# A recurrence stage written one projection ahead, with its first two projections in half pieces and 360-column third pieces

## The chip, the cores and the metric

The kernel runs on one core of a Trainium2 chip. The metric is the device time of one launch in microseconds (us); lower is better. Matmuls run on TensorE (PE), elementwise work on VectorE (DVE), ScalarE (ACT) and GpSimd (POOL), and transfers are issued from the queues of SyncE (SP) and of ACT.

## What is computed

One layer of a hybrid decoder for 1024 prompt tokens and 8 sequences of 8 sample tokens, width 1024. The part that matters here is the first branch:

```
xn = rms_norm(x, norm_g)
proj = jnp.einsum('btd,dn->btn', xn, w_in)
x_lru, z_lru, q, k, v, z_gla, a_lo, gate_logits = jnp.split(proj, IN_SPLITS, axis=-1)
xc, conv_new = causal_conv(x_lru, conv0, conv_w, conv_b)
# rg_lru: r, i = sigmoid(block-diagonal maps of xc); a = exp(-8 r softplus(-lam))
# h_t = a_t h_(t-1) + sqrt(1 - a_t^2) (i_t xc_t)
y_a = jnp.einsum('btw,wd->btd', h.astype(dt) * jax.nn.silu(z_lru), w_lru_o)
```

A gated linear attention branch, a merge of the two, an output projection and a last norm follow. They are untouched, except that their projections use the same helper `piece`.

## The kernel before

**Layout.** Channels lie on the 128 partitions, tokens along the free dimension: 1088 tokens, padded to 1092, in 3 pieces of 364 columns. A projection ("job") makes 128 output channels for all tokens. Each fp32 operand is kept as a high and a low part, so a job is 3 pieces x 8 k-steps x 3 products (L455 to L457) = 72 matmuls. There are 72 jobs: 16 in the recurrence stage, 16 in the first merge stage, 24 in the attention, 16 after it. Only 16 of the jobs, x(i) and z(i) for the 8 channel blocks i, belong to the recurrence stage.

**Weights.** Of each weight block, ACT makes the high part (`hi`, L817, semaphore hi_ok) and POOL the low part (`lo`, L423, semaphore lo_ok); there are two slots, even jobs in slot 0 and odd ones in slot 1. POOL runs its program in order: `lo(0, 0)` for x(0), then the masks and constants of the attention (L429 to L444), then `lo(0, 1)` for z(0), then the rest in a loop.

**Start.** For nine tiles of tokens ACT squares and takes the root (L827, L830), DVE scales (L1133), PE transposes (`x_transpose`, L482, 8 per tile), ACT and DVE split into high and low (L837, L1124). PE runs in order; between the transposes it puts pieces of x(0). z(0) starts after x(0) is complete.

**Recurrence stage.** Two banks of three PSUM slots: bankA for x(i) and then the r gate, bankB for z(i) and then the i gate. PE per block: z(i), gates(i) (two gates of 9 matmuls, L455 to L457 on xcs), x(i+1). The gates need the convolution of x(i): ACT copies x(i) out of bankA (`evacuate`, L860 to L862), DVE convolves (L1186, L1189), ACT and DVE split the result (L870, L1197). DVE also copies z(i) out (L1199). Then come the tanhs, decay, root, scan (L874 to L886, L1201 to L1229) of block i.

## Time and profile before

| | us |
|---|---|
| median of 3 runs | 1186.61 |
| lowest and highest | 1181.58, 1188.57 |
| the profiled execution, its own time | 1186.15 |
| its span, first to last instruction | 1184.4 |
| TensorE busy within the span | 1149.3 |

TensorE is busy nearly throughout; the recurrence stage takes from about 43 us to 259 us. A row of the timeline gives start, duration, engine, line, operation, and in brackets how long the engine was idle before and what ended that. Matmuls overlap in their recorded durations, so the rate of a run of matmuls is the distance of their starts.

### The profile page before, as it was taken

To read this page: it belongs to the slowest core of one execution; us is meant where nothing else is said; L and a number is where in the kernel's file an instruction comes from. 1 tells how busy PE (TensorE), PEld (TensorE's weight loads), DVE (VectorE), ACT (ScalarE), POOL (GpSimd) and SP (SyncE) were. 2 spreads that over 40 slices of the span, in tenths; PEclk is the share of its full clock that TensorE was granted. 3 is DMA by queue.
4 is the path that set the end of the run, shared out by engine and by line. 5 is a ranking of instruction groups with operands and counts; after the bars stand their busy time and mean duration, and the time that the engine had idled before them with its cause. 6 is when DMAs were issued, how large, how long until landed. Compare 5 with 4: busy or idle time off the path is not lost.

```text
span 1184.4 us, 17796 instructions
## 1 busy us (share of the span) xinstructions
PE 1149.3 (97%) x6888; PEld 1108.4 (94%) x6888; DVE 540.2 (46%) x711; ACT 423.5 (36%) x557; POOL 199.2 (17%) x128
## 2 busy tenths in 40 slices
PE   5899999999999999999999999999999999999997
PEld 5899999999999999999999999999989999999886
DVE  5777777775000001662395357438534002444332
ACT  5555555554111112542543453345434111122211
POOL 3511111111212120210112011111202121120000
PEclk8999999999999999998999999999999999999999
DMA  6211111111211222210311131031002103432331
GB/s 210 65 41 49 48 40 40 40 36 37 91 55 54 72 75 64 68 37 18 112 35 35 35 95 35 18 96 52 18 18 80 49 18 110 154 117 90 107 106 54
DMA packets 95488, 76.18 MB, mean 64 GB/s; under 512 B 3928, under 2 KB 88792, under 8 KB 95464
## 3 DMA queue, kind: packets, MB, share of 16 engines
q1 hardware_dynamic: 84444, 61.59, 17.5%
q10 hardware_dynamic: 11020, 14.26, 3.5%
q8 instruction: 16, 0.26, 0.1%
q14 instruction: 8, 0.07, 0.0%
HBM read 62.04 MB, written 13.80 MB: 64 GB/s over the span
## 4 chain that ended last, share of the span: by engine, by line
PE 88%; issue 6%; DVE 3%; ACT 2%; DMA 0%; DVEq 0%; ACTq 0%
PE ps L455 26%; PE ps L456 25%; PE ps L457 25%; PE ps L590 2%; PE ps L653 1%; PE ps L632 1%; PE ps L624 1%; PE ps L634 1%; PE ps L617 1%; DVE xcs L1197 1%; PE ps L672 1%; ACT xcs L870 1%; PE ps L561 1%; DVE xc L1189 1%; PE ps L581 1%
## 5 line engine op out<-in xcount | busy, mean ns | idle before, releaser
L455 PE MATMUL ps<-xn,whi 128*128 128x364 f32 x1344 | 451.9, 336 | 1.7 <-DVE xn L1124 1.5
L456 PE MATMUL ps<-xn,whi 128*128 128x364 f32 x1344 | 443.1, 330 | 0.0
L457 PE MATMUL ps<-xn,wlo 128*128 128x364 f32 x1344 | 442.7, 329 | 0.0
L423 POOL TENSOR_TENSOR wlo<-raw,whi 128x1024 fp32r<-128x1024 f32 x72 | 180.9, 2513 | 860.6 <-ACT whi L817 860.6
L455 PEld LDWEIGHTS ps<-xn,whi 128*128 128x128 f32 x1344 | 254.0, 189 | 6.1 <-issue 2.5
L456 PEld LDWEIGHTS ps<-xn,whi 128*128 128x128 f32 x1344 | 254.2, 189 | 0.2
L457 PEld LDWEIGHTS ps<-xn,wlo 128*128 128x128 f32 x1344 | 253.7, 189 | 0.0
L817 ACT ACTIVATE whi<-raw 128x1024 fp32r<-128x1024 f32 x72 | 76.0, 1056 | 151.6 <-PE ps L457 85.9
L456 PE MATMUL ps<-act_s,whi 128*128 128x364 f32 x384 | 126.2, 329 | 0.0
L455 PE MATMUL ps<-act_s,whi 128*128 128x364 f32 x384 | 126.2, 329 | 0.0
L457 PE MATMUL ps<-act_s,wlo 128*128 128x364 f32 x384 | 126.1, 329 | 0.0
L1245 DVE SCALAR_TENSOR_TENSOR keep<-keep,ps 128x1092 f32 x7 | 9.0, 1292 | 146.6 <-PE ps L457 146.6
L1427 DVE TENSOR_TENSOR wos<-woraw,wos 128x1024 f32 (+1 forms) x8 | 18.4, 2304 | 124.3 <-ACT wos L1078 124.3
L457 PEld LDWEIGHTS ps<-act_s,wlo 128*128 128x128 f32 x384 | 72.2, 188 | 0.0
L456 PEld LDWEIGHTS ps<-act_s,whi 128*128 128x128 f32 x384 | 72.2, 188 | 0.0
L455 PEld LDWEIGHTS ps<-act_s,whi 128*128 128x128 f32 x384 | 72.1, 188 | 0.0
L456 PE MATMUL ps<-wos,whi 128*128 128x512 f32 x144 | 56.0, 389 | 0.0
L455 PE MATMUL ps<-wos,whi 128*128 128x512 f32 x144 | 56.0, 389 | 0.0
L457 PE MATMUL ps<-wos,wlo 128*128 128x512 f32 x144 | 56.0, 389 | 0.0
L1308 DVE COPY_PREDICATED att<-lmask,ps 128x256 f32<-128x256 uint16 x56 | 26.1, 531 | 25.1 <-PE ps L590 25.1
L1107 ACT ACTIVATE junk<-yy 128x1024 f32<-128x1024 f32 (+1 forms) x9 | 9.5, 1060 | 75.9 <-DVE yy L1469 75.9
L1189 DVE SCALAR_TENSOR_TENSOR xc<-xbuf,vec,xc 128x1024 f32<-128x1024 f32 (+1 forms) x48 | 34.6, 779 | 0.0
(230 smaller groups left out, 1367.2 us busy)
## 6 DMA issues: line engine op xcount, KB each, us to landing
raw<-in_w_in SPq DMA_DIRECT2D x56, 512.0 KB, 3.8
branch_a<-keep ACTq DMA_DIRECT2D x8, 546.0 KB, 2.8
mal<-branch_a SPq DMA_DIRECT2D x8, 544.0 KB, 4.6
xt<-in_x_prompt SPq DMA_DIRECT2D x8, 512.0 KB, 6.8
raw<-in_w_lru_o SPq DMA_DIRECT2D x8, 512.0 KB, 3.6
st<-in_state_gla ACTq DMA_DIRECT2D x4, 1024.0 KB, 5.5
out<-st ACTq DMA_DIRECT2D x4, 1024.0 KB, 4.7
raw<-in_w_gla_o SPq DMA_DIRECT2D x8, 512.0 KB, 5.7
```

What stands on the lines that cost most here:

```text
L423: pool.tensor_tensor(wlo[:, c % 2], raw[:, c % 2], whi[:, c % 2].bitcast(F32), ALU.subtract).then_inc(s["lo_ok"], 1)
L455: pe.matmul(dst, wh, mh, start=first, stop=False)
L456: pe.matmul(dst, wh, ml, start=False, stop=False)
L457: return pe.matmul(dst, wl, mh, start=False, stop=last)
L561: ins = pe.matmul(ps[0:2 * RANK, bankA + j, 0:PIECE], aw[:, k, :], xn[:, r, k, j * PIECE:(j + 1) * PIECE], start=(k == 0 and r == 0), stop ...
L581: ins = pe.matmul(ps[:, b, c * P:(c + 1) * P], kb[:, cols], qb[:, cols], start=True, stop=True)
L590: ins = pe.matmul(ps[:, b, i * P:(i + 1) * P], qk[:, l % 2, 2 * i * P:(2 * i + 1) * P], qk[:, l % 2, (2 * i + 1) * P:(2 * i + 2) * P], sta ...
L617: ins = pe.transpose(ps[0:nr, b, (n % 4) * P:(n % 4 + 1) * P], src[:, n * P:n * P + nr], ident[:, :])
L817: act.activation(whi[:, c % 2], raw[:, c % 2], ACT.Copy).then_inc(s["hi_ok"], 1)
L1189: ins = dve.scalar_tensor_tensor(dst, src, wk, dst, ALU.mult, ALU.add)
L1308: ins = dve.copy_predicated(dst, mask, src)
L1427: dve.tensor_tensor(wos[:, 1, 2 * i + j, :], woraw[:, :], wos[:, 0, 2 * i + j, :].bitcast(F32), ALU.subtract).then_inc(s["wo_lo"], 1)
```

## The change

PE's order per block becomes x(i+1), gates(i), z(i+1), with the i gate ahead of the r gate in the loop; ACT and DVE follow with functions for each part, called for block i and i+1 in turn. The last block is written out after the loop, on ACT as z_tanh(7), decay_root(6), hi, r_gate_tanh(7), i_gate_tanh(7). The copy of z out of PSUM is gone: ACT's tanh and DVE's silu read bankB directly. At the start PE interleaves half pieces of x(0) and z(0) with the transposes; the loads of the small rows move from SP's queue to ACT's; z(0)'s weights are loaded and split (`hi(0, 1)`) earlier. POOL's program is the same. The third piece of every job and gate has 360 columns in place of 364.

```diff
+        def columns(j):
+            return slice(j * PIECE, min((j + 1) * PIECE, NTOK))
...
@@ sync
-            sp.wait_ge(s["pad_ok"], 1)
-            row(R_CONVW, t["conv_w"][0])
...
+            sp.wait_ge(s["x_sq"], 1)
+            load_x(4)
+            sp.dma_start(raw[:, 1], w_in[:, :, COL_Z:COL_Z + P]).then_inc(s_raw[1], 16)
+            for n in range(5, TTILES):
...
@@ tensor
-            x_transpose(4)
-            pe.wait_ge(s["lo_ok"], 1)
-            piece(0, bankA, xn, 0)
+            FIRST, SECOND = range(KT // 2), range(KT // 2, KT)
+            pe.wait_ge(s["x_lo"], 3)
+            pe.wait_ge(s["lo_ok"], 1)
+            piece(0, bankA, xn, 0, FIRST)
+            x_transpose(4)
+            piece(0, bankA, xn, 0, SECOND)
             x_transpose(5)
+            pe.wait_ge(s["lo_ok"], 2)
+            piece(1, bankB, xn, 0, FIRST)
             x_transpose(6)
+            piece(1, bankB, xn, 0, SECOND)
+            x_transpose(7)
             pe.wait_ge(s["x_lo"], 6)
-            piece(0, bankA, xn, 1, range(KT // 2))
-            x_transpose(7)
+            piece(0, bankA, xn, 1, FIRST)
             x_transpose(8)
-            piece(0, bankA, xn, 1, range(KT // 2, KT))
+            piece(0, bankA, xn, 1, SECOND)
+            pe.wait_ge(s["x_lo"], TTILES - 1)
+            piece(1, bankB, xn, 1)
             pe.wait_ge(s["x_lo"], TTILES)
...
             piece(0, bankA, xn, 2).then_inc(s["job_done"], 1)
+            piece(1, bankB, xn, 2).then_inc(s["job_done"], 1)
...
             with pe.Fori(0, KT - 1) as i:
-                z_and_gates(i)
-                pe.wait_ge(s["r_tanh"], i + (ONE + 1))
+                pe.wait_ge(s["x_evac"], i + 1)
+                pe.wait_ge(s["r_tanh"], i + ONE)
                 job(i, N_LRU + 2, bankA, xn)
-            z_and_gates(KT - 1)
+                gate_pair(i, i + 2, (1, 0))
+                pe.wait_ge(s["i_tanh"], i + (ONE + 1))
+                job(i, N_LRU + 3, bankB, xn)
+            gate_pair(KT - 1, KT, (0, 1))
...
@@ scalar
+            act.wait_ge(s["pad_ok"], 1)
+            row(R_CONVW, t["conv_w"][0])
...
+                if n == 3:
+                    hi(0, 1)
...
+            def act_step(i):
+                act.wait_ge(s["job_done"], 2 * i + 3)
+                evacuate_x(i + 1)
+                i_gate_tanh(i)
+                r_gate_tanh(i)
+                hi(i, 4)
+                gate_hi(i + 1)
+                decay(i)
+                conv_hi(i + 1)
+
+            with act.Fori(0, KT - 2) as i:
+                act_step(i)
+                decay_root(i)
+                z_tanh(i + 1)
+                hi(i, 5)
+            act_step(KT - 2)
+            z_tanh(KT - 1)
+            decay_root(KT - 2)
+            hi(KT - 2, 5)
+            r_gate_tanh(KT - 1)
+            i_gate_tanh(KT - 1)
+            decay(KT - 1)
+            decay_root(KT - 1)
...
@@ vector
+            with dve.Fori(0, KT - 2) as i:
+                gated_input(i)
+                conv(i + 1)
+                input_scale(i)
+                conv_lo(i + 1)
+                recurrence(i, sz)
+                z_silu(i + 1, sz)
+            gated_input(KT - 2)
+            conv(KT - 1)
+            conv_lo(KT - 1)
+            input_scale(KT - 2)
+            z_silu(KT - 1, tz)
+            recurrence(KT - 2, sz)
+            gated_input(KT - 1)
```

**First place: PE at the start.** Before, with the semaphores that a row waits for (lo_ok counts the low weight parts from POOL, x_scaled and x_lo the token tiles; a 128x364 matmul row opens a run of them):

```order
L492 MATMUL ps<-ident,rows 128x44 [waits rows_in]
...
L482 MATMUL ps<-ident,xt 128x128 [waits x_lo,x_scaled]
L482 MATMUL ps<-ident,xt 128x128 x7
L455 MATMUL ps<-xn,whi 128x364 [waits lo_ok]
...
L455 MATMUL ps<-xn,whi 128x364 [waits x_lo]
...
L482 MATMUL ps<-ident,xt 128x64 [waits x_lo,x_scaled]
...
L455 MATMUL ps<-xn,whi 128x364 [waits pad_ok,x_lo]
```

The same stretch after the change, where the second row with lo_ok is the first one of z(0):

```order
L490 MATMUL ps<-ident,rows 128x44 [waits rows_in]
...
L453 MATMUL ps<-xn,whi 128x364 [waits lo_ok,x_lo]
...
L480 MATMUL ps<-ident,xt 128x128 [waits x_lo,x_scaled]
L480 MATMUL ps<-ident,xt 128x128 x7
L453 MATMUL ps<-xn,whi 128x364 [waits lo_ok]
...
L453 MATMUL ps<-xn,whi 128x364 [waits x_lo]
...
L480 MATMUL ps<-ident,xt 128x64 [waits x_lo,x_scaled]
...
L453 MATMUL ps<-xn,whi 128x360 [waits vec_ok,pad_ok,x_lo]
```

The wait for z(0)'s low weights (the second lo_ok) moved from behind all nine transposes and all of x(0) to ahead of the transposes 6, 7 and 8 and of two thirds of x(0).

**Second place: PE in the loop of the recurrence stage.** Before, from the gates (xcs) of block i to x(i+1):

```order
L455 MATMUL ps<-xcs,ghi 128x364 [waits g_lo,xc_lo]
...
L455 MATMUL ps<-xcs,ghi 128x364 [waits z_copy]
...
L468 REGISTER_ALU [waits r_tanh]
L455 MATMUL ps<-xn,whi 128x364 [waits lo_ok]
...
L526 COMPARE_AND_BRANCH
```

After, one turn of the loop, x(i+1), the gates, and z(i+1):

```order
L466 ISA [waits r_tanh,x_evac]
L453 MATMUL ps<-xn,whi 128x364 [waits lo_ok]
...
L527 REGISTER_ALU [waits g_lo,xc_lo]
L453 MATMUL ps<-xcs,ghi 128x364 [waits z_silu]
...
L453 MATMUL ps<-xcs,ghi 128x364 [waits r_tanh,x_evac]
...
L466 REGISTER_ALU [waits i_tanh]
L453 MATMUL ps<-xn,whi 128x364 [waits lo_ok]
```

x(i+1) moved between the evacuation of x(i) and the gates that need its convolution; the second gate now waits for the evacuation of x(i+1).

**Third place: ACT at the end of the stage.** Before, the last turn of the loop is like every other (tr and ti are the gates' tanhs, xcs the high part of the convolution, wt<-wt the root):

```order
L870 ACTIVATE xcs<-xc 128x1092 [waits conv_step]
L816 REGISTER_ALU [waits raw_in1]
L817 ACTIVATE whi<-raw 128x1024 [waits job_done]
L874 ISA [waits r_done,dvec_ok]
L874 ACTIVATE tr<-ps,dvec 128x1092
```

After, from the high part of block 7's convolution to the tanh of its r gate:

```order
L894 ACTIVATE xcs<-xc 128x1092 [waits conv_step]
L900 ACTIVATE tz<-ps 128x1092 [waits z_silu,job_done]
L921 ACT_TABLE_LOAD
L921 ACTIVATE wt<-wt 128x1092 [waits w_ok]
L828 ACTIVATE whi<-raw 128x1024 [waits job_done,raw_in1]
L910 ACT_TABLE_LOAD
L910 ACTIVATE tr<-ps,dvec 128x1092 [waits r_done]
```

The tanh of z, the root of block 6 and two table loads now stand ahead of the tanh of block 7's r gate.

## Rows read from the trace of the kernel before

**Rows 1.** The page, busy time and share of the span, engine PE

```profile
PE 1149.3 (97%) x6888; PEld 1108.4 (94%) x6888; DVE 540.2 (46%) x711; ACT 423.5 (36%) x557; POOL 199.2 (17%) x128
```

**Rows 2.** Timeline of PE, one turn of the loop: start us, duration us, operation

```profile
88.29 0.32 PE L456 MATMUL ps<-xn,whi 128*128 128x364 f32 x1
...
111.91 0.33 PE L457 MATMUL ps<-xn,wlo 128*128 128x364 f32 x1
113.20 0.43 PE L455 MATMUL ps<-xcs,ghi 128*128 128x364 f32 x1 [0.96 <-DVE xcs L1197]
...
116.14 0.33 PE L457 MATMUL ps<-xcs,glo 128*128 128x364 f32 x1
116.46 0.43 PE L455 MATMUL ps<-xn,whi 128*128 128x364 f32 x1
```

**Rows 3.** Timeline of ACT, the same turn

```profile
100.44 1.28 ACT L860 ACT_TABLE_LOAD   x1 [5.12 <-PE ps L457]
101.74 0.78 ACT L860 ACTIVATE xbuf<-ps 128x728 f32<-128x728 f32 x1
...
102.71 0.23 ACT L862 ACTIVATE xbuf<-ps 128x64 f32<-128x64 f32 x1
...
116.61 1.17 ACT L877 ACTIVATE ti<-ps,dvec 128x1092 f32<-128x1092 f32 x1 [0.28 <-PE ps L457]
...
122.67 1.12 ACT L886 ACTIVATE wt<-wt 128x1092 f32<-128x1092 f32 x1 [0.20 <-DVE wt L1207]
```

**Rows 4.** Windows, that turn: PE, PEld, DVE, ACT, POOL busy us, clock, DMA

```profile
84.70:113.20 28.50, 27.48 (x162) 26.88 (x162) 21.04 (x27) 14.07 (x16) 4.81 (x2) 1.00 0.15 41
```

**Rows 5.** Timeline of POOL and DVE at the start

```profile
17.11 2.97 POOL L423 TENSOR_TENSOR wlo<-raw,whi 128x1024 fp32r<-128x1024 f32 x1 [13.92 <-ACT whi L817]
...
22.52 1.29 DVE L1133 SCALAR_TENSOR_TENSOR xt<-xt,rstd,ngb 128x1024 f32<-128x1024 f32 x1
...
22.68 1.23 POOL L430 TENSOR_SCALAR_AFFINE_SELECT lmask<-lmask 128x64 bf16<-128x64 bf16 x1
```

**Rows 6.** Timeline of POOL, the low weight part of z(0)

```profile
40.80 2.41 POOL L423 TENSOR_TENSOR wlo<-raw,whi 128x1024 fp32r<-128x1024 f32 x1
```

**Rows 7.** Timeline, DVE and ACT at the start; ACT queue at 463 us

```profile
1.12 0.91 DVE L1115 MEMSET rows<- 44x1024 f32 x1 [0.18 <-issue]
...
6.22 1.06 ACT L827 ACTIVATE junk<-xt 128x1024 f32<-128x1024 f32 x1 [3.45 <-DMA xt<-in_x_prompt]
...
15.98 1.04 ACT L817 ACTIVATE whi<-raw 128x1024 fp32r<-128x1024 f32 x1
...
463.46 2.70 ACTq L963 DMA_DIRECT2D wa_raw<-in_w_a  x6
```

**Rows 8.** Timeline of PE at the start

```profile
24.19 0.51 PE L456 MATMUL ps<-xn,whi 128*128 128x364 f32 x1
24.49 0.51 PE L457 MATMUL ps<-xn,wlo 128*128 128x364 f32 x1
...
28.59 1.91 PE L482 MATMUL ps<-ident,xt 128*128 128x128 f32 x16
...
43.27 0.43 PE L455 MATMUL ps<-xn,whi 128*128 128x364 f32 x1 [0.20 <-POOL wlo L423]
```

**Rows 9.** Windows of PE: stretch, busy us, granted clock, DMA share, GB/s

```profile
26.40:26.60 0.20, 0.20 (x3) 0.63 0.00 0
1180.00:1181.00 1.00, 0.00 (x0) 0.63 0.00 0
```

**Rows 10.** Timeline of PE, the end of the stage: last z(7), first merge projection

```profile
254.17 0.33 PE L457 MATMUL ps<-xn,wlo 128*128 128x364 f32 x1
...
258.64 0.43 PE L455 MATMUL ps<-xn,whi 128*128 128x364 f32 x1
```

**Rows 11.** Timeline of PE, matmuls of 512 columns, the output projection

```profile
1099.98 0.39 PE L456 MATMUL ps<-wos,whi 128*128 128x512 f32 x1
...
1102.93 0.39 PE L457 MATMUL ps<-wos,wlo 128*128 128x512 f32 x1
```

More of the change, by code:

```diff
@@ L230, in build, with part_of @@
         bankA, bankB = 0, 3
-        bankX, bankR = (3, 6), 5
+        bankX, bankR = (slice(6, 8), slice(4, 6)), 2
+        def columns(j):
+            return slice(j * PIECE, min((j + 1) * PIECE, NTOK))
+        def part_of(b, j):
+            return ps[:, b + j, 0:columns(j).stop - columns(j).start]
         def slot3(b):
@@ L324, in _ @@
         def _(sp):
-            def row(r, ap):
-                sp.dma_start(rows[r:r + ap.shape[0], 0:ap.shape[1]], ap).then_inc(s["rows_in"], 16)
             def load_x(n):
@@ L507, in _, with gate_pair @@
             piece(0, bankA, xn, 2).then_inc(s["job_done"], 1)
-            pe.wait_ge(s["vec_ok"], 1)
-            def z_and_gates(i):
-                pe.wait_ge(s["i_tanh"], i + ONE)
-                job(i, N_LRU + 1, bankB, xn)
+            piece(1, bankB, xn, 2).then_inc(s["job_done"], 1)
+            def gate_pair(i, evacuated, gates):
                 pe.wait_ge(s["xc_lo"], i + 1)
                 pe.wait_ge(s["g_lo"], i + 1)
-                for g, b in ((0, bankA), (1, bankB)):
-                    if g == 1:
-                        pe.wait_ge(s["z_copy"], i + 1)
+                for g in gates:
+                    b = (bankA, bankB)[g]
+                    if g == 0:
+                        pe.wait_ge(s["x_evac"], evacuated)
+                        pe.wait_ge(s["r_tanh"], i + ONE)
+                    else:
+                        pe.wait_ge(s["z_silu"], i + (ONE + 1))
@@ L1115, in _ @@
             dve.memset(rows[:, :], 0.0).then_inc(s["pad_ok"], 1)
-            dve.memset(xn[:, :, :, NTOK:TOK].bitcast(F32), 0.0).then_inc(s["pad_ok"], 1)
+            dve.memset(xn[:, :, :, NTOK:TOK].bitcast(F32), 0.0)
+            dve.memset(ps[:, bankA + 2:bankB + 3:3, NTOK - 2 * PIECE:PIECE], 0.0).then_inc(s["pad_ok"], 1)
             dve.wait_ge(s["ng_in"], 16)
```

96 lines of the change are left out of this document (60 added, 36 removed).

## The prediction

> **What bounds the kernel now.** I read the busy shares first: TensorE (PE) is busy 97% of the span, no other engine half of it [rows 1]. So a change gains only where PE stands still or where its instructions get shorter. Then I read PE's timeline for gaps. One turn of the recurrence loop has two. The gates start 1.29 us after the last matmul of z(i), where neighbours start 0.166 us apart (142 steps from 88.29 to 111.91), and the reason given is the low part of the convolution; x(i+1) starts 0.32 us after the last gate [rows 2]. With about 0.1 us lost on the first matmul after each wait, a turn takes 28.45 us (the window of rows 4 is one) against 162 x 0.1664 = 26.96 us of matmuls. So the loop has 1.5 us a turn to give. DVE is busy 21.0 us and ACT 14.1 us of a turn [rows 4]: both have room. Then I read the start, where the order of POOL and PE decides, and the end of the stage, where the change writes out another order.
>
> **The change, part by part.**
>
> Loop. x(i+1), 12 us of matmuls, now lies between the convolution of block i and the gates that need it, so the 1.29 us wait goes. What is late next? Let t be the start of the last matmul of x(i+1). The i gate follows at t+0.17, 9 matmuls, last at t+1.5. ACT starts 0.47 us after PE's last matmul starts (116.14 to 116.61 [rows 2, 3]). Its table load of 1.28 us before the evacuation is gone, since the turn now ends in a tanh and the order of the instructions has no load there. The evacuation takes 1.20 us (101.74 to 102.94 [rows 3]), so it ends at t+1.7 and PE sees it at about t+1.9. The r gate could have started at t+1.67: a stall of 0.2 us. It ends at t+3.4. The tanh of the i gate runs t+2.0 to t+3.2 (1.17 us [rows 3]), just in time for z(i+1) in the same bank. z ends at t+15.4 and the next x at t+27.4 less 54 narrower matmuls x 1.6 ns = 0.1 us. I take a turn of 27.2 to 27.3 us. From the last z(0) matmul to the last z(7) matmul are 7 turns: 254.17 - 55.2 = 199.0 us before [rows 10, 8], 190.4 us after. **Loop: -8.6 us** (bounds: -10 with no stall at all, -6 with 0.4 us more a turn).
>
> What hides the rest: DVE does gated input, convolution, scaling, low part, recurrence and silu in series, 21.0 us less the removed copy of 1.3 us, plus some 1.5 us of waiting for the root; it starts at t+3.2 and must have the silu of z(i+1) by t+27. That leaves about 3 us or more. If the cover were gone, each us would cost 7 us in all. ACT's decay, root and weight split end near t+18.
>
> End of the stage. Before, the last z(7) matmul starts at 254.17 and the merge stage at 258.64: 4.47 us [rows 10]. After, with T for that matmul: ACT's tanh of z runs T+0.5 to T+1.7, DVE's silu (1.3 us like its other full-width steps) to T+3.0, and only then may the i gate write bankB; the r gate fills T+0.2 to T+1.7. Meanwhile ACT goes on with a table load (1.28), the root of block 6 (1.12 [rows 3]), a weight split (1.04 [rows 7]), another table load (1.28), and only then the tanh of r (1.17), each overlapping the next by about 0.1: it ends at T+7.5. The first merge projection needs bankA, which that tanh reads: it starts at T+7.6. **End: +3.1 us** (bounds +2 to +4). The y projection behind two merge projections keeps its cover: its operands come about 0.6 us later than before, relative to the merge stage, with 24 us of matmuls ahead of it.
>
> Start. This is the large term. POOL's program is the same: x(0)'s low part at 17.11, then masks, then z(0)'s low part from 40.80 to 43.21 [rows 5, 6]. Before, z(0) began at 43.27 and waited 0.2 us for it [rows 8]: hidden behind x(0). After, PE waits for it behind transposes 0 to 5 and one piece of x(0), which are done near 30 us. Queued behind the wait are transposes 6, 7 and 8, two pieces of x(0) and all of z(0); and ACT and DVE wait for the transposes. PE stands still for some 14 us.
> When does the weight come? The loads of the small rows now precede ACT's first square, at 6.22 before. They start after the memset at 2.03; six such issues on ACT's queue take 2.70 us, so ten take 4.5, then a table load and a root 1.5: 8.0, that is 1.8 later [rows 3, 7]. SP-like prices would give 0.5. I take 1.5, being nearer to the row of the same queue. The first weight split, 15.98, hangs on this chain [rows 7], POOL on it, and the masks on POOL. Against this, a mask beside DVE's scaling took 1.23 us and ended 0.1 us after it [rows 5]; one such scaling falls behind the wait: -0.5. So PE goes on at 43.2 + 1.5 - 0.5 = 44.2 (bounds 42.5 to 46).
> A rule of the Trainium skill bears on that pair. SBUF — State Buffer, Who interferes with whom: a VectorE instruction with two SBUF inputs and a GpSimd one that reads SBUF exclude each other, whoever comes later waiting for the other's end. The mask's row agrees. If the rule held for every scaling that meets a mask, all of POOL's list would end up to 3 us sooner in a kernel whose DVE is idle; only one scaling is idled here.
> After the wait: five pieces of 24 matmuls, 120 x 0.1664 = 20.0; two transposes at half of 1.91 us [rows 8] and the half-wide one 0.64: 2.5; first matmuls after waits 0.4. The last z(0) matmul then starts at 44.2 + 22.7 = 66.9.
> PE's clock comes on top. At the start matmuls came 0.30 us apart (24.19, 24.49 [rows 8]), the 1.2 GHz level, until the granted clock rose at about 26.5, after some 3.6 us of matmuls. At the end of the kernel it fell near 1180.3, with PE idle since 1176.8 [rows 9]. 14 us idle should drop it. Twelve matmuls at 0.30 and one transpose at double cost 1.6 + 0.7, and a little until the rise: 2.4 us (bounds 0 to 4). So 69.3 against 43.27 + 11.9 = 55.2. **Start: +14.1 us** (bounds +11 to +17). The weights and evacuation for x(1) follow x(0), which ends 4 us before z(0); split 1.04, POOL 2.41 and 0.5 of handoff just fit, so x(1) does not wait.
> A second rule speaks against this change: TensorE: Matmul & The Clock Gate, Loop structure matters more than you think, says that a PE that waits long between matmuls runs the next ones cold. By that rule the 2.4 us are due; if the clock stayed up the total would be 2.4 us less. The row of the kernel's end agrees.
>
> Narrower pieces. 512 columns start 0.227 us apart (13 steps from 1099.98 to 1102.93 [rows 11]), 364 columns 0.1664: 0.41 ns a column, 1.6 ns for four. Outside the stage 56 jobs x 24 = 1344 such matmuls: **-2.2 us**; zero if time comes in coarser steps.
>
> The split of x_lo in two, the added memset and the missing copy of z lie on DVE beside idle time: nothing.
>
> **Sum.** +14.1 - 8.6 + 3.1 - 2.2 = +6.4 us on the profiled execution's 1186.15, which is 0.5 below the median of 1186.61: 1193.0 as a median.
>
> **The rivals.**
> A, the other side: the wait for z(0)'s weights does not bind, and the interleaving does what it looks like. It decides at about 29 us: if the low part is there by then, PE runs through, some 3 us of idle PE at the start go, the last z(0) matmul is at 52, and the sum is -3 - 8.6 + 3.1 - 2.2 = -10.7: 1176. For it only that each piece is ready sooner; against it POOL's row at 40.80 with the same program. Chance 0.06.
> B, the wait binds but is cheap: masks run faster while DVE idles, and the clock rises at once. Resumption near 42, +10.5 at the start: 1189.5. Against it, DVE is busy through most of the masks. Chance 0.12.
> C, the loop does not get shorter: if the evacuation, the i gate's tanh or DVE's longer chain is late, each turn keeps a wait of 1.2 us in the new places. It decides when DVE needs more than 24 us from the i gate's tanh to the next silu. The sum is +15: 1201.5. Chance 0.07.
> D, the end is worse: 3 us idle, a few matmuls and 1.3 us idle before them drop the clock again, +2.5: 1195.5. Chance 0.05.
>
> **How the numbers follow.** Main case 0.70, 1193.0, own range 1190.5 to 1195.5. 0.5% of the median is 5.9 us, about what a measurement tells from no change: the border is at 1192.5. The main case lies just above it, 0.55 of it beyond: slower 0.39 + C 0.07 + D 0.05 = 0.51; same 0.31 + B 0.12 = 0.43; faster 0.06. The range 1188.5 to 1198.5 leaves out A, C and edges.
>
> **What would show it.** In the changed profile: PE idle from about 30 to 44 us with POOL's weight part as the releaser, transposes 6 to 8 after it, and granted clock 0.5 behind it; the last z(0) matmul near 69. Turns of 27.2 us with no wait above 0.3 us. Two waits after z(7), for DVE's silu and ACT's tanh, and 7.6 us to the merge stage. Third pieces 0.1648 us apart. Wrong if PE resumes before 42, if ACT's first square comes at 6.5, or if turns stay above 28.

## The result, and the profile after

The changed kernel takes 1192.22 us (median of 20 runs, 1189.82 to 1196.79) against 1185.42 us of the kernel before in the same runs: the ratio is 1.0062, 95% interval 1.005 to 1.0073, some 7 us slower. The forecast was 1193.0 as a median. The profiled execution took 1194.07 us in all, its span 1192.4.

The page of the changed kernel, PE's line and the line of the x, z and merge matmuls' group (busy us, mean ns, idle us before it and its main releaser), answering to [rows 1]:

```profile
PE 1147.6 (96%) x6888; PEld 1108.8 (93%) x6888; DVE 543.5 (46%) x713; ACT 422.0 (35%) x556; POOL 205.0 (17%) x128
...
L453 PE MATMUL ps<-xn,whi 128*128 128x364 f32 (+1 forms) x1344 | 453.0, 337 | 17.5 <-POOL wlo L421 15.0
```

PE is busy 96% of the span, and of that group's 17.5 us of idle time 15.0 are one releaser's, POOL's low weight. PE's timeline of the changed kernel at the start (start us, duration us, operation, idle time and its releaser); it answers to [rows 8]:

```profile
28.40 1.04 PE L480 MATMUL ps<-ident,xt 128*128 128x128 f32 x8
44.43 0.67 PE L453 MATMUL ps<-xn,whi 128*128 128x364 f32 x1 [14.99 <-POOL wlo L421]
...
48.23 1.42 PE L480 MATMUL ps<-ident,xt 128*128 128x128 f32 x8
49.41 0.41 PE L453 MATMUL ps<-xn,whi 128*128 128x364 f32 x1
...
68.95 0.32 PE L455 MATMUL ps<-xn,wlo 128*128 128x360 f32 x1
```

PE stands for 15 us behind the transposes, and the releaser is POOL's low weight. Twelve matmuls run at a step of 0.30 us there (0.46 the first), and the last matmul of z(0) starts at 68.95, where 69.3 was forecast. The windows of PE across the wait (stretch, its length, busy us and matmuls, granted clock, DMA share, GB/s), which answer to [rows 9]:

```profile
30.00:32.00 2.00, 0.00 (x0) 0.99 0.00 0
32.00:34.00 2.00, 0.00 (x0) 0.50 0.00 0
...
44.00:49.00 5.00, 4.57 (x16) 0.50 0.01 3
49.00:50.00 1.00, 1.00 (x10) 0.99 0.00 0
```

The clock went to its 1.2 GHz level near 32.0 us, 2.6 us after PE's last transpose ended, and back to 2.4 GHz some 4.6 us after it resumed. Why the weight came when it did is in the timelines of ACT and POOL, which answer to [rows 7] and [rows 6]:

```profile
6.02 1.28 ACT L842 ACT_TABLE_LOAD   x1 [6.02 <-issue]
...
7.43 1.04 ACT L848 ACTIVATE junk<-xt 128x1024 f32<-128x1024 f32 x1
...
17.17 1.04 ACT L828 ACTIVATE whi<-raw 128x1024 fp32r<-128x1024 f32 x1
```

```profile
42.03 2.34 POOL L421 TENSOR_TENSOR wlo<-raw,whi 128x1024 fp32r<-128x1024 f32 x1
```

ACT's ten row loads end at 6.02, its first square starts 1.2 us later than before, and so do the first weight's high part and, behind the masks, z(0)'s low weight. One turn of the loop, PE's timeline, answering to [rows 2]:

```profile
109.59 0.32 PE L455 MATMUL ps<-xcs,glo 128*128 128x360 f32 x1
109.81 0.44 PE L453 MATMUL ps<-xcs,ghi 128*128 128x364 f32 x1
...
111.25 0.32 PE L455 MATMUL ps<-xcs,glo 128*128 128x360 f32 x1
111.50 0.43 PE L453 MATMUL ps<-xn,whi 128*128 128x364 f32 x1
...
135.47 0.32 PE L453 MATMUL ps<-xcs,ghi 128*128 128x364 f32 x1
...
137.00 0.44 PE L453 MATMUL ps<-xcs,ghi 128*128 128x364 f32 x1
```

The i gate of the next turn starts at 135.47. From the r gate at 109.81 to the next at 137.00 is a turn of 27.19 us. The r gate starts 0.22 us after the matmul ahead of it and z(i+1) 0.25 us, where the regular step is some 0.165: no stall in the turn is over 0.1 us. Its window, answering to [rows 4]:

```profile
109.64:136.83 27.19, 27.19 (x164) 26.79 (x162) 21.51 (x25) 14.02 (x16) 5.33 (x2) 1.00 0.15 43
```

The end of the stage, answering to [rows 10]:

```profile
259.17 0.33 PE L455 MATMUL ps<-xn,wlo 128*128 128x360 f32 x1
...
262.29 0.43 PE L453 MATMUL ps<-xcs,ghi 128*128 128x364 f32 x1 [1.31 <-DVE tz L1274]
...
266.53 0.44 PE L453 MATMUL ps<-xn,whi 128*128 128x364 f32 x1 [2.49 <-ACT tr L910]
```

From the last z(7) matmul to the merge stage it is 7.36 us, with waits for DVE's silu and for ACT's tanh of r.

**Where the 7.9 us of the two profiled executions went.** Last z(0) matmul +13.8 (68.95 against 55.18). Seven turns: 190.22 against 198.99, -8.8. End of the stage: 7.36 against 4.47, +2.9. From the merge stage to the transposes of the tails (which start at 459.16, before at 450.53): +0.7. From there to the last matmul (1184.26, before 1176.37): -0.7. The last two are narrower pieces and stretches of the lower clock: one of 3.4 us from 267.5 costs 1.6 us (twelve matmuls 0.30 us apart), and both kernels have others among the 8-column matmuls of the attention heads, at 555 to 568 us and 665 to 675 us before, at 565 to 575, 670 to 682 and 885 to 895 us after (windows of PE of the changed kernel, columns as above):

```profile
268.00:270.50 2.50, 2.50 (x9) 0.50 0.72 206
670.00:682.00 12.00, 11.51 (x49) 0.57 0.00 0
```

Which heads have one differs between these two traces, and the 20 runs of the kernel before lie 9 us apart; that the one makes the other is argued, not shown. So below I read each experiment at a mark ahead of the heads too: **the start of the transposes of the tails**, 450.53 before and 459.16 after.

The stations of every trace on the way to the mark, with the start of the last matmul of z(0) and of z(7), of the merge stage, and of the first y projection (us; in the last column where the granted clock fell to its 1.2 GHz level after 240 us):

| | last z(0) | last z(7) | merge | y | mark | clock fell at |
|---|---|---|---|---|---|---|
| before | 55.18 | 254.17 | 258.64 | 282.70 | 450.53 | |
| changed | 68.95 | 259.17 | 266.53 | 292.06 | 459.16 | merge |
| e1 | 52.34 | 242.56 | 249.93 | 276.65 | 443.93 | |
| e2 | 56.60 | 246.78 | 254.14 | 280.86 | 449.56 | y |
| e3 | 69.38 | 259.60 | 264.32 | 296.67 | 466.61 | y |
| e4 | 69.60 | 260.53 | 267.89 | 293.51 | 461.34 | merge |
| e5 | 51.35 | 241.52 | 248.89 | 274.40 | 441.51 | merge |
| e6 | 52.53 | 242.71 | 247.43 | 273.96 | 441.25 | |
| e7 | 68.70 | 258.87 | 263.59 | 291.62 | 461.04 | y |
| e8 | 67.07 | 257.29 | 264.65 | 290.19 | 457.30 | merge |
| e9 | 51.77 | 241.98 | 246.68 | 270.54 | 438.98 | |
| e10 | 67.31 | 257.48 | 264.85 | 290.36 | 457.46 | merge |
| e11 | 56.04 | 253.50 | 258.00 | 281.98 | 449.08 | |
| e12 | 51.55 | 241.93 | 254.91 | 279.95 | 447.05 | last gate |

Kernels with the same program up to z(7) lie up to 1.2 us apart there (e1, e5, e6, e9, e12), so a difference of 1 us at the mark tells nothing. The times were taken in three groups: the kernel before took 1185.88 us in the runs of e1 to e4, 1183.30 in those of e5 to e8 and 1183.14 in those of e9 to e12, against 1185.42 in the changed kernel's. Across groups I go by the ratios.

### The profile page after: what moved, and what is told of

The parts are those of the page before. It is cut to its first block, busy times and chain, and to the rows that moved or that the text cites. A ratio compares the mean times of both kernels' runs of the same rounds, so it can differ in the third digit from the quotient of the medians.

```text
span 1192.4 us, 17729 instructions
## 1 busy us (share of the span) xinstructions
PE 1147.6 (96%) x6888; PEld 1108.8 (93%) x6888; DVE 543.5 (46%) x713; ACT 422.0 (35%) x556; POOL 205.0 (17%) x128
## 4 chain that ended last, share of the span: by engine, by line
PE 95%; POOL 2%; ACT 1%; issue 1%; DVE 1%; ACTq 0%; DVEq 0%; POOLq 0%
PE ps L453 28%; PE ps L454 27%; PE ps L455 27%; PE ps L601 2%; PE ps L664 1%; PE ps L643 1%; PE ps L635 1%; PE ps L645 1%; PE ps L628 1%; PE ps L683 1%; PE ps L572 1%; PE ps L592 1%; POOL lmask L430 1%; POOL lmask L428 1%; POOL wlo L421 0%
## 5 line engine op out<-in xcount | busy, mean ns | idle before, releaser
L453 PE MATMUL ps<-xn,whi 128*128 128x364 f32 (+1 forms) x1344 | 453.0, 337 | 17.5 <-POOL wlo L421 15.0
L455 PE MATMUL ps<-xn,wlo 128*128 128x364 f32 (+1 forms) x1344 | 443.5, 330 | 0.0
L454 PE MATMUL ps<-xn,whi 128*128 128x364 f32 (+1 forms) x1344 | 443.2, 330 | 0.0
L421 POOL TENSOR_TENSOR wlo<-raw,whi 128x1024 fp32r<-128x1024 f32 x72 | 186.8, 2594 | 862.2 <-ACT whi L828 862.2
L453 PEld LDWEIGHTS ps<-xn,whi 128*128 128x128 f32 x1344 | 255.2, 190 | 21.1 <-POOL wlo L421 15.2
L454 PE MATMUL ps<-act_s,whi 128*128 128x364 f32 (+1 forms) x384 | 125.9, 328 | 0.0
L455 PE MATMUL ps<-act_s,wlo 128*128 128x364 f32 (+1 forms) x384 | 125.9, 328 | 0.0
L453 PE MATMUL ps<-act_s,whi 128*128 128x364 f32 (+1 forms) x384 | 125.8, 328 | 0.0
L1258 DVE SCALAR_TENSOR_TENSOR xc<-xbuf,vec,xc 128x1024 f32<-128x1024 f32 (+1 forms) x48 | 51.8, 1139 | 0.0
```

The source lines that it names most:

```text
L421: pool.tensor_tensor(wlo[:, c % 2], raw[:, c % 2], whi[:, c % 2].bitcast(F32), ALU.subtract).then_inc(s["lo_ok"], 1)
L453: pe.matmul(dst, wh, mh, start=first, stop=False)
L454: pe.matmul(dst, wh, ml, start=False, stop=False)
L455: return pe.matmul(dst, wl, mh, start=False, stop=last)
L1258: ins = dve.scalar_tensor_tensor(dst, src, wk, dst, ALU.mult, ALU.add)
```

## The experiments

**e1: z(0)'s low weight ahead of the masks.** POOL makes both first low weights before its masks.

```
             lo(0, 0)
+            lo(0, 1)
             for l, m in enumerate(LEVELS):
...
-            lo(0, 1)
             with pool.Fori(1, (N_YB + KT) // 2) as i:
```

> The changed kernel with one move on POOL: the low part of z(0)'s weights ahead of the attention's masks. Theory 1 (the wait for that weight at the start is the large term): PE's wait of 15.0 us and the clock's fall behind it go; the last z(0) matmul comes at 52 to 54 us in place of 69, and the time is 15 to 17 us below the changed kernel's 1192.2, that is 9 us below the kernel before. Rival (the weight is only the first of several things late at the start: tiles, or x(1)'s weights behind the moved masks, keep PE waiting): PE waits 5 us or more in new places and the time stays at 1181 or above.

1178.44 us, ratio to before 0.9938 (0.9908 to 0.9967); mark 443.93, 15.2 us ahead of the changed kernel's. The wait of 15 us is gone, the last z(0) matmul starts at 52.34, and PE has no wait over 0.3 us from z(0) to the end of the loop. So one line in POOL's order is the whole difference between slower and faster than before. But a wait of 2.6 us, ahead of the first y projection, is new. PE's timeline there, and ACT's:

```profile
273.73 0.32 PE L455 MATMUL ps<-xn,wlo 128*128 128x360 f32 x1
276.65 0.41 PE L453 MATMUL ps<-act_s,whi 128*128 128x364 f32 x1 [2.60 <-DVE act_s L1332]
```

```profile
267.78 6.15 ACT L961 ACTIVATE act_s<-keep  x6 [4.50 <-DVE keep L1304]
273.94 1.28 ACT L964 ACT_TABLE_LOAD   x1
275.24 1.17 ACT L964 ACTIVATE keep<-ps,dvec 128x1092 f32<-128x1092 f32 x1
```

The trace names DVE as the releaser, but the tanh of the first merge gate, which empties the banks that y writes, ended at 276.41, 0.24 us ahead of the matmul, behind six copies and a table load. Of DVE's low parts the first y matmul needs one only, and six were made from 269.17 on in 7.33 us, so that the first was there some 6 us earlier. e5 and e7 take up the same question. DVE and POOL of e1 show what made the copies late:

```profile
264.26 3.30 DVE L1304 TENSOR_TENSOR keep<-hh,tz 128x1092 f32<-128x1092 f32 x1
```

```profile
263.36 3.05 POOL L421 TENSOR_TENSOR wlo<-raw,whi 128x1024 fp32r<-128x1024 f32 x1 [13.39 <-ACT whi L828]
```

The last kept part (keep 7, the gated output of block 7; keep 6 is that of block 6), 1.30 us long in the changed kernel (at 280.85), took 3.30 us here, begun while POOL was subtracting.

**e2: PE's start in the order of before**, the rest as changed (x(0) between the transposes as before, then z(0) as one job; the hunk is the one of `FIRST, SECOND` in the diff).

> The changed kernel with PE's order at the start as in the kernel before (all of x(0), then z(0)); the loop, the end, the narrow pieces and the row loads on ACT stay. Theory 1: the last z(0) matmul is back at 55 to 57 us (1 us later than before for the row loads on ACT), so the time is 12.5 to 14 us below the changed kernel: 1179, 6 us below the kernel before. Rival (the new loop or its end loses the time): 1188 or above.

1179.78 us, ratio 0.995 (0.9931 to 0.997); mark 449.56. As theory 1 said, within 1 us. At the last z(7) matmul e2 is 4.2 us behind e1: with the weight in time, the interleaved start is worth having, though the times of e1 and e2 are not told apart; with POOL's masks ahead of it, it costs 12.4 us at the same place (9.6 at the mark: e2 takes 1.2 us more from the merge stage to y, where it waits, and 1.6 more from y to the mark, where its clock was down at first).

**e3: the last r gate's tanh ahead of the root of step 6.**

```
             z_tanh(KT - 1)
+            r_gate_tanh(KT - 1)
             decay_root(KT - 2)
             hi(KT - 2, 5)
-            r_gate_tanh(KT - 1)
             i_gate_tanh(KT - 1)
```

> The changed kernel with one line moved: in the block that is written out after the loop, ACT's tanh of the r gate stands ahead of the root of block 6. Theory 1 (ACT's order there holds the bank that the merge stage needs): from the last z(7) matmul to the merge stage 4.6 us in place of 7.5, and the clock does not fall behind it, which cost 12 matmuls at 0.30 us, 1.6 us more: 4 to 4.7 us less than the changed kernel, 1188. Rival (the later root delays block 6 and with it the y projection): the wait moves to the y projection and at most 1 us is left.

1199.27 us, ratio 1.0112 (1.0084 to 1.014); mark 466.6: a miss by 11 us, in the wrong direction. The merge stage did start 4.72 us behind the last z(7) matmul instead of 7.36, but the y projection then waited 8.34 us. ACT's timeline of e3:

```profile
263.93 1.12 ACT L921 ACTIVATE wt<-wt 128x1092 f32<-128x1092 f32 x1
...
272.58 1.28 ACT L906 ACT_TABLE_LOAD   x1 [6.59 <-DVE keep L1304]
...
287.82 6.13 ACT L961 ACTIVATE act_s<-keep  x6 [6.54 <-DVE keep L1304]
...
295.26 1.17 ACT L964 ACTIVATE keep<-ps,dvec 128x1092 f32<-128x1092 f32 x1
```

The root comes 2.0 us later than in the changed kernel (261.93 there), the tanh of i now needs a table load of its own after its wait (272.58), and the copies of the kept parts start at 287.82 instead of 282.37. The third part of these 5.4 us is DVE beside POOL: the 128x8 add of recurrence 7 took 2.29 us (281.49, POOL subtracting from 281.35), 0.17 in the changed kernel. After the wait the clock was down, and from y to the mark e3 takes 2.8 us longer than the changed kernel. What ends last at the end of this stage is not the merge stage's start but a chain: recurrence 6, tanh of i, recurrence 7, copies, and the first merge gate's tanh.

**e4: third pieces of 364 columns again.** `columns` returns `slice(j * PIECE, (j + 1) * PIECE)`.

> The changed kernel with third pieces of 364 columns again. If the cost of a matmul goes with its columns at 1.6 ns for four, 1344 matmuls outside the recurrence stage and 432 in it are 2.9 us slower: 1195.1. If time comes in coarser steps: no difference. A run-to-run spread of some 3 us may hide it in the medians; then the distance of starts in the third pieces decides (0.1667 against 0.1642).

1195.8 us, ratio 1.009 (1.0065 to 1.0116): 3.6 us more than the changed kernel in the medians, with intervals that overlap (1.005 to 1.0073), so the time alone does not show it. The traces do. From the first y matmul to the mark lie 14 jobs with 336 third-piece matmuls: 167.83 us with 364 columns (before, e4), 167.10 with 360 (changed, e10, e11). That is 2.2 ns each, not 1.6, and the steps between 300 and 450 us say the same: 166.5 ns at 364 columns and 164.3 at 360.

**e5: on e1, four of the six copies moved into ACT's idle time.**

```
             act.activation(aw[:, :, 0:RANK], araw[:, :, :], ACT.Copy).then_inc(s["alo_hi"], 1)
+            act.wait_ge(s["i_x"], KT)
+            act.wait_ge(s["x_tail"], KT + ONE)
+            act.wait_ge(s["hz_ok"], 4 + ONE)
+            for k in range(4):
+                act.activation(act_s[:, 0, k, :], keep[:, k, :], ACT.Copy).then_inc(s["act_hi"], 1)
             hi(0, N_MIXA + 2)
             act.wait_ge(s["hz_ok"], KT + ONE)
...
-            with act.Fori(0, KT - 2) as i:
...
+            for k in range(4, KT - 2):
...
```

> The kernel of e1, with four of the six ACT copies of kept parts 0 to 3 into act_s moved ahead, into the time in which ACT waits for the last recurrence (in e1 ACT waits 1.83 us and 4.50 us there). e1 had a wait of 2.6 us ahead of the first y projection, which its trace puts down to DVE's act_s at L1332; the copies stood at 267.78, six in 6.15 us, then a table load of 1.28 us and the tanh of the first merge gate (L964), which ended at 276.41, 0.24 us before the projection's first matmul at 276.65. Theory 1: it was this tanh that was waited for, since it empties the banks that the projection writes to. Four copies less ahead of it are 4.1 us, more than the 2.6 us: the wait is gone, 1178.44 - 2.6 = 1175.8 us. Rival: DVE's low parts were waited for, as the trace says; they can start 1.5 us earlier (at the end of the last keep instead of behind the first copy), so 1.1 us of wait are left: 1176.9 us, and the first act_s matmul stands 1.1 us behind the one before it.

1175.52 us, ratio 0.9933 (0.9908 to 0.9958); mark 441.51, 2.4 us ahead of e1's, 1.0 us of it already at the last z(7) matmul. By the ratios, 0.9933 against 0.9938, it is not told apart from e1. No wait is left ahead of y, as theory 1 has it: the merge gate's tanh ends 22.2 us after the merge stage began, in e1 26.5, with y due at some 24. But the edit does more than shorten the row of copies (4.1 us). They now stand ahead of the weight copy `hi(0, N_MIXA + 2)`, so POOL's subtraction begins at 264.38, behind the last kept part, which takes 1.29 us again (2.0 us); it meets a small copy of DVE instead, and ACT waits 1.99 us for DVE's first low part. So e5 shows that the chain to this tanh was waited for, and not that the copies alone were the reason.

**e6: on e5, a buffer of its own for the last i gate.** The last i gate's tanh goes to the first half of xcs (`ti7`), so it need not wait for recurrence 6; two copies are early.

```
             z_tanh(KT - 1)
+            r_gate_tanh(KT - 1)
             decay_root(KT - 2)
             hi(KT - 2, 5)
-            r_gate_tanh(KT - 1)
-            i_gate_tanh(KT - 1)
+            act.wait_ge(s["i_done"], KT + ONE)
+            act.activation(p3(ti7[:, :]), slot3(bankB), ACT.Tanh, ...)
+            act.wait_ge(s["h_ok"], KT - 1)
             decay(KT - 1)
...
-            gated_input(KT - 1)
             dve.wait_ge(s["h_tail"], KT - 1)
             input_scale(KT - 1)
-            recurrence(KT - 1, tz)
+            gated_input(KT - 1, ti7[:, :])
+            recurrence(KT - 1, tz, ti7[:, :])
```

> The kernel of e5 with the end of the stage rewritten: the last r gate's tanh goes ahead of the square root of step 6 (as in e3), but the last i gate's tanh writes into the first half of xcs, which is free by then, and so no longer waits for the recurrence of step 6 to be done with ti; the exponential waits for the scan of step 6 alone; the last gated input is made behind the input scale, beside ACT's root; two copies are early, not four. Theory 1 (the chain recurrence 6, gate tanh, recurrence 7, copies, merge tanh sets when y can start): merge stage starts right behind the last i gate, at about 247.3 us instead of 249.93 in e1; root 6 at 246.7, keep 6 done at 253, exponential at 251.7, root 7 at 255.5, keep 7 done at about 262 (267.6 in e1), merge tanh done at 268.4 where y wants its banks at 271.4: no wait. 1178.44 - 2.6 - 2.6 = 1173.2 us. Rival: the end of the stage is bound by the count of table loads and by DVE and POOL in each other's way, as in e3: the y projection then waits what the merge stage gained, and the time stays at e5's 1175.8 or above.

1174.35 us, ratio 0.9915 (0.9891 to 0.9938); mark 441.25, level with e5's. The merge stage started with no wait, as forecast, but the y projection waited 2.52 us: keep 7 was done at 267.0, not 262. The timelines of DVE and POOL in e6 have the two instructions that took the difference (249.52 and 263.76), each begun while POOL was subtracting:

```profile
249.52 2.25 DVE L1306 TENSOR_TENSOR ti<-ti,fix 128x8 f32<-128x8 f32 x1
...
261.05 0.18 DVE L1306 TENSOR_TENSOR ti<-ti,fix 128x8 f32<-128x8 f32 x1
...
263.76 3.31 DVE L1312 TENSOR_TENSOR keep<-hh,tz 128x1092 f32<-128x1092 f32 x1
```

```profile
249.18 2.56 POOL L422 TENSOR_TENSOR wlo<-raw,whi 128x1024 fp32r<-128x1024 f32 x1 [12.49 <-ACT whi L829]
262.79 3.12 POOL L422 TENSOR_TENSOR wlo<-raw,whi 128x1024 fp32r<-128x1024 f32 x1 [11.05 <-ACT whi L829]
```

The same instruction of 128x8 elements takes 2.25 us beside POOL and 0.18 us alone.

**e7: e3 with the four copies of e5.** (Both diffs above.)

> The kernel of e3 (last r gate's tanh ahead of the root of step 6) with the four copies moved ahead as in e5. In e3 the y projection waited 8.34 us, to 296.67; the merge gate's tanh ended there at 296.43, behind copies that started at 287.82 (6.13 us) and a table load. Theory 1: the wait falls by four copies, 4.1 us, to 4.2 us: 1199.27 - 4.1 = 1195.2 us, and less the clock that stays up more of that time, about 0.5 us. Rival (low parts of DVE waited for): only 1.5 us less, 1197.8 us.

1193.8 us, ratio 1.008 (1.0055 to 1.0104); mark 461.04, 5.6 us ahead of e3's. The wait fell from 8.34 to 4.01 us, by about the 4.1 us of the copies, though as in e5 POOL's subtraction moved too (the 128x8 add takes 0.18 us again, and ACT waits 1.99 us for a low part). With less of the wait left the trace now names the releaser that was meant all along:

```profile
291.62 0.65 PE L453 MATMUL ps<-act_s,whi 128*128 128x364 f32 x1 [4.01 <-ACT keep L968]
```

**e8: PE kept at work through the wait.** 80 matmuls without use, into a bank nobody reads.

```
             x_transpose(5)
+            pe.wait_ge(s["vec_ok"], 1)
+            for _ in range(80):
+                pe.matmul(ps[:, bankR, 0:352], whi[:, 0, 0, :], xn[:, 0, 0, 0:352], start=True, stop=True)
             pe.wait_ge(s["lo_ok"], 2)
```

> The changed kernel with 80 matmuls without use (364 by 128, 352 columns each, into a bank that nobody reads) between the sixth transposition of x and the wait for z(0)'s low weight, so that TensorE works through 12 of the 15 us that it waits there. Everything else waits as before. Theory 1: the wait itself stays (POOL's low weight at 44.4 us) but the granted clock is still at its upper level when it ends: the 12 matmuls that took 0.30 us each take 0.17, and the transpositions between them their usual time: 2.0 to 2.5 us less, 1189.9 us. Rival: the clock had no part in the 14 us, since work behind the wait had slack: 1192.2 us as before.

1190.02 us, ratio 1.0049 (1.0024 to 1.0074), which is not told apart from the changed kernel's 1.0062; mark 457.30, 1.9 us ahead, although the useless matmuls ran 0.3 us too long (z(0) at 44.74 instead of 44.43). PE's timeline of e8:

```profile
44.74 0.33 PE L453 MATMUL ps<-xn,whi 128*128 128x364 f32 x1
...
46.74 1.04 PE L480 MATMUL ps<-ident,xt 128*128 128x128 f32 x8
47.53 0.41 PE L453 MATMUL ps<-xn,whi 128*128 128x364 f32 x1
```

The stretch up to the second half of z(0)'s first piece takes 2.79 us, with the clock down, in the changed kernel, 4.98: the clock's price is 2.2 us.

**e9: on e6, two weight copies moved** so that POOL does not subtract while DVE's chain runs.

```
             z_tanh(KT - 1)
+            hi(KT - 2, 5)
             r_gate_tanh(KT - 1)
             decay_root(KT - 2)
-            hi(KT - 2, 5)
...
-            hi(0, N_MIXA + 2)
             act.wait_ge(s["hz_ok"], KT + ONE)
...
+            hi(0, N_MIXA + 2)
             act.wait_ge(s["job_done"], N_MIXA + 1)
```

> The kernel of e6 with two ACT weight copies moved, and with them the POOL subtractions that they start. In e6 two DVE instructions of the last recurrences took 2.25 us instead of 0.18 (128x8, at 249.52) and 3.31 us instead of 1.29 (keep, at 263.76), each begun while POOL subtracted a low weight, and the y projection still waited 2.52 us for the merge gate's tanh. The copy for part 5 of step 6 now stands ahead of the last r gate's tanh, so that POOL works while DVE waits for ACT's root; the copy for the first merge projections stands behind the kept parts' copies. Theory 1 (such an overlap with POOL costs DVE some 2 us each, on the chain that y waits for): the root comes 0.65 us later, the two stretched instructions are gone (4.1 us), keep 7 is done at about 263.5 (267.0 in e6), the wait of 2.52 us is gone or under 0.5: e6's 1174.35 - 2.4 = 1172 us. Rival: the stretch moves with the copies to other DVE instructions of the chain: the wait stays 2 to 2.5 us and the time that of e6.

1173.82 us, ratio 0.9921 (0.9906 to 0.9937); mark 438.98, 2.3 us ahead of e6's, 0.7 of it already at the last z(7) matmul. In the trace theory 1 holds: DVE's keep 7 takes 1.29 us and is done at 262.7, and y starts with no wait at 270.54 (273.96 in e6); PE waits 0.3 and 0.4 us inside it for low parts. The timed runs don't tell e9 from e6. DVE's last kept part in e9:

```profile
261.37 1.29 DVE L1312 TENSOR_TENSOR keep<-hh,tz 128x1092 f32<-128x1092 f32 x1
```

**e10: the ten row loads issued from SP again.**

```
-            act.wait_ge(s["pad_ok"], 1)
-            row(R_CONVW, t["conv_w"][0])
...
             load_x(3)
+            sp.wait_ge(s["pad_ok"], 1)
+            row(R_CONVW, t["conv_w"][0])
...
             sp.wait_ge(s["x_sq"], 1)
```

> The changed kernel with its ten small row loads issued from SP again, between the x and weight loads, instead of from ACT. In the changed kernel ACT issues them from 2.07 to 6.00 us, and its first square begins at 7.43 us instead of 6.22. Theory 1: z(0)'s low weight, which PE waits for, stands behind that square through the x operands, the first weight's high part, POOL's subtraction and 21 mask steps, so all of it moves 1.2 us: PE resumes at 43.2 instead of 44.4 us, 1191.0 us. Rival: SP's x loads, which the rows now delay by about 4 us, pace the start instead; then the x transpositions 4 to 8 come later, but all before 43 us, so PE resumes at 43.2 all the same, and z(0)'s first half only is met by x(8); or the first operands don't move at all and the time stays at 1192.2.

1189.85 us, ratio 1.007 (1.0045 to 1.0096), mark 457.46. ACT's first square starts at 6.14 us and PE resumes at 43.19, 1.24 us sooner, as theory 1 had it to the tenth:

```profile
43.19 0.67 PE L463 MATMUL ps<-xn,whi 128*128 128x364 f32 x1 [13.77 <-POOL wlo L431]
```

The time can't tell: the median is 2.4 us lower, the ratio no lower than the changed kernel's 1.0062. The mark is 1.7 us ahead, 1.2 of it the wait's.

**e11: before, with the 360-column third pieces alone.**

```
+        def columns(j):
+            return slice(j * PIECE, min((j + 1) * PIECE, NTOK))
...
-                    cols = slice(j * PIECE, (j + 1) * PIECE)
+                    cols = columns(j)
```

> The kernel of before with one part of the change alone: third pieces of 360 columns in the x, z, gate, merge, y and branch projections. The prediction took 2.2 us for this part; undone in the changed kernel (e4) it cost 3.6 us. Theory 1: it is the columns alone, 0.1667 us a matmul against 0.1642, with no waits in play: the time is 2.2 to 3.6 us under that of before. Rival: in before the loop is paced by its waits, so the narrower pieces of the recurrence loop give nothing there and only the later stages count: 1.5 us or less.

1182.27 us against 1183.14 of before in the same runs, ratio 0.9985 (0.9967 to 1.0004): between nothing and 3.9 us, so neither theory is excluded. The trace shows that the loop keeps its wait for xcs (1.01 to 1.03 us a turn) and a turn of 28.4 us; the mark is 1.45 us ahead of before's.

**e12: on e1, the written-out last step back in the loops.**

```
-            with act.Fori(0, KT - 2) as i:
+            with act.Fori(0, KT - 1) as i:
                 act_step(i)
                 decay_root(i)
                 z_tanh(i + 1)
                 hi(i, 5)
-            act_step(KT - 2)
-            z_tanh(KT - 1)
-            decay_root(KT - 2)
-            hi(KT - 2, 5)
...
-            with dve.Fori(0, KT - 2) as i:
+            with dve.Fori(0, KT - 1) as i:
...
-            recurrence(KT - 1, tz)
+            recurrence(KT - 1, sz)
```

> The kernel of e1 (its start mended) with the written-out last step put back into the loops: ACT and DVE run step 6 as they run steps 0 to 5 (DVE's input scale ahead of the low half of xc, ACT's root ahead of z's tanh, z's silu into sz behind recurrence 6), and step 7 uses sz. Worked out from e1's trace: the root of step 6 begins at 242.5 instead of 245.3, keep 6 is done at 249.0 instead of 253.8, z(7)'s silu at 250.3 instead of 245.6, so the last i gate runs from 250.3 to 252 and the merge stage starts at 252 (249.93 in e1); the i gate's tanh starts at 252 instead of 253.94. Theory 1 (the y projection's start, not the merge stage's, is where the end of the stage is felt): y can start 1.9 us earlier than in e1, at 274.8, but the merge projections end only at 276.1, so it starts there without a wait: 1178.44 - 0.5 = 1177.9 us; the order written out for the last step is worth nothing. Rival (the merge stage's start counts, as the prediction's sum had it): 2.1 us more, 1180.5 us.

1179.52 us, ratio 0.9962 (0.9946 to 0.9978); mark 447.05, 3.1 us behind e1's. PE's timeline of e12:

```profile
244.74 0.32 PE L455 MATMUL ps<-xcs,glo 128*128 128x360 f32 x1
252.02 0.67 PE L453 MATMUL ps<-xcs,ghi 128*128 128x364 f32 x1 [6.96 <-DVE sz L1270]
...
254.91 0.51 PE L453 MATMUL ps<-xn,whi 128*128 128x364 f32 x1
```

The wait for the silu was 1.7 us longer than forecast, since keep 6 stood beside POOL (3.14 us), and after 7 us without work the clock was down, which cost another 2.3 us up to the y projection, at 279.95 (27.9 us behind the i gate's start, where e1's own matmuls from i gate to y take 25.6). So the written-out order is worth some 3 us at the mark against the loop's order (3.7 counted from the last z(7) matmul), while the times, 0.9962 against 0.9938, are not told apart; my first theory, that it is worth nothing, is wrong, and the rival's 2.1 us is nearer, though not for its reason alone.

## Why the prediction was right, by its steps

**The start** was forecast at +14.1 and is +13.8. Each link is in the rows: the square 1.2 us later (1.5 taken), the weight's end at 44.37 (44.2 taken), the clock's 2.4 us (e8: 2.2). e1 shows the cause by itself: with the weight in time the 15 us are gone. e10 shows the part of the row loads, 1.24 us. The -0.5 for a mask freed from DVE's scaling is not there: the weight's end moved by 1.16 us (43.21 to 44.37), as much as the square. One mask fewer was held up (four, before five), but POOL's list from the first mask to the weight took as long as before (21.27 to 42.03, before 20.02 to 40.80): by the lengths of their neighbours the masks lost 3.6 us in both. So the 1.5 was 0.3 too large and the -0.5 some 0.45, and their sum came out near. In the clock's 2.4 the transpose was put at 0.7 us, and its start to the next matmul's is 0.4 longer than in e8.

**DVE beside POOL** mattered less at the start than the prediction had it, and more in the loop and at the end of the stage, where the prediction has no term for it. In e6 a 128x8 add with two SBUF inputs waited 2.1 us for a POOL subtraction, and with the subtractions moved (e9) keep 7 was done 4.4 us sooner and y started 3.4 us sooner (3.7 and 2.7, counted from the merge stage's start). By the Trainium skill, SBUF — State Buffer, Who interferes with whom, a VectorE instruction with two SBUF inputs and a GpSimd one that reads SBUF exclude each other; the rows of e6 agree.

**The loop**: -8.6 forecast, -8.8 found, with a turn of 27.19 us; the stall ahead of the r gate was put at 0.2 us and is under 0.1. DVE's slack was put at about 3 us; its silu of z ends at 133.46, and the i gate that needs it starts at 135.47, 2.0 us later. Here too the missing part is POOL, which subtracts from 128.06 to 130.98. DVE's timeline of the changed kernel:

```profile
128.92 3.20 DVE L1304 TENSOR_TENSOR keep<-hh,sz 128x1092 f32 x1
...
132.18 1.28 DVE L1274 SCALAR_TENSOR_TENSOR sz<-tz,ps 128x1092 f32<-128x1092 f32 x1
```

At the mark e2, with only the start undone, is 1.0 us ahead of before, and that adds up: +1.4 at the last z(0) matmul, -8.8, +2.9, +2.7 from the merge stage's start to y, +0.9 from y to the mark. The time says 6.1 us (3.6 to 8.2 by the ratio's interval). Behind the mark the narrow pieces give some 2.1 us; the other 3 are not accounted for.

**The end of the stage**: +3.1 forecast, +2.9 found (7.36 us). The terms that the forecast lists, less their overlaps, end the tanh at T+7.1 to T+7.2, not at T+7.5; it ended at T+7.3. But the sentence after it was wrong, the y projection does not keep its cover in the sense said. Its operands were to come 0.6 us later relative to the merge stage. What lets y start is ACT's first merge gate tanh, before and after:

```profile
279.39 1.18 ACT L899 ACTIVATE keep<-ps,dvec 128x1092 f32<-128x1092 f32 x1
```

```profile
289.83 1.18 ACT L964 ACTIVATE keep<-ps,dvec 128x1092 f32<-128x1092 f32 x1
```

Before, it ended 21.9 us after the merge stage began (280.57 less 258.64), with y due at 24.1. After, it ends at 24.5 (291.01 less 266.53), 2.6 us later, not 0.6: the cover was some 2 us and is used up. The step left out recurrence 6, which in the changed order is still running when the merge stage begins, and which the i gate's tanh waits for; and in it, DVE beside POOL. The timelines of DVE and POOL in the changed kernel:

```profile
264.41 2.20 DVE L1298 TENSOR_TENSOR ti<-ti,fix 128x8 f32<-128x8 f32 x1
...
278.15 0.17 DVE L1298 TENSOR_TENSOR ti<-ti,fix 128x8 f32<-128x8 f32 x1
```

```profile
264.07 2.50 POOL L421 TENSOR_TENSOR wlo<-raw,whi 128x1024 fp32r<-128x1024 f32 x1 [10.93 <-ACT whi L828]
```

This one add holds 2.0 of the 2.6 us. In e1 and e2 the last kept part meets POOL as well, 2.0 us more, and y waits 2.6 us; in e3 there are a later root, a table load and another such add, and y waits 8.3. e5 and e9 remove the wait by shortening that chain, e7 half of it.

**Narrower pieces**: the term was mis-sized. 2.2 ns a matmul instead of 1.6 makes 3.0 us outside the stage instead of 2.2 (and 1 us in the loop, which its turn of 27.19 already has). At the mark e4 is 2.2 us late, where 816 such matmuls stand ahead of it, 1.8 us. The 1.6 came from a line through 364 and 512 columns; a step so near 364 can't be read from it.

**The rival of the clock at the end** (2.5 us, chance 0.05) came about in the profiled execution with 1.6 us: its mechanism was given too little chance. Of the seven traces with this end of the stage and its two waits, the clock fell in five (changed, e4, e5, e8, e10) and stayed up in e1 and e2, so it comes and goes. But it does not add up as the rival has it. Where it fell, y started 25.5 to 25.6 us after the merge stage without a wait (changed, e4, e8, e10), and where it stayed up, 26.7 us after it (e1, e2; 24.1 before). The rows say why: the weight copy that starts POOL's subtraction waits for a merge projection. With slower projections it came so late (POOL at 281.52) that the last kept part had begun (280.85) and took 1.30 us. So the fall cost 1.6 us of matmuls and saved a wait of 2.6, of which the rival and the prediction had neither.

**The sum.** Of the 7.9 us between the profiled executions the forecast's terms give 1.5 less than it took for them (start -0.3, loop -0.2, end -0.2, narrow pieces -0.8), and 3.0 came that it did not have: 1.6 from the clock's fall at 267.5, and 1.4 behind the mark, beyond the narrow pieces, which I put down to the clock in the heads without having shown it. The nearness of the whole (+6.4 forecast, +6.8 between the medians) rests partly on luck.

**The rival on the other side** (1176, chance 0.06) was the right picture of what the change would do with its weight in time: e1, 1178.44, with the last z(0) matmul at 52.34 where it had 52. What kept it from happening is what the prediction said, POOL's masks. Its 1176 left out the y projection's wait of 2.6 us.

## What to carry to other kernels

When a change makes a tuned engine ask for an operand earlier, follow that operand back through every queue it stands in, and read the other engines' unchanged programs for when it comes; here a helper's list of masks, harmless before, cost 15 us, and one moved line turned a loss of 7 us into a gain of 7. When a stage hands over to the next, the start of the first job of the next stage is not yet the end: look for the next operand with little cover, and for what its releaser waits for in turn; the wait's named releaser is the nearest in time, and the program's own semaphore counts tell which was meant; moving work off one candidate (e5, e7) helps, if one looks at what else the move shifts. The best of these kernels by its median, e9 at 1173.82 us (e5 and e6 are not told from it), is 9.3 us faster than before and takes the changed loop and start, the weight first, and a shorter last step.
